# Two weight tiles side by side after each norm, one-column root sums, and the scan's preparation shared between VectorE and GpSimd

## The reference, cut to what matters

```python
def rms_norm(x, g):
    y = x * lax.rsqrt(jnp.mean(x * x, axis=-1, keepdims=True) + NORM_EPS)
    return y * g
h = rms_norm(x, g_pre_mix[l]) * (1.0 + sc1) + sh1
y, yc = token_mixer(h, hc, p, rope_hd, rope_mla, not last)
x = x + gt1 * rms_norm(y, g_post_mix[l])
h = rms_norm(x, g_pre_mlp[l]) * (1.0 + sc2) + sh2
x = x + gt2 * rms_norm(sq_relu_mlp(h, w_mlp1[l], w_mlp2[l]), g_post_mlp[l])
```

```python
w_log = -softplus(-(w0[d] + wt @ w2[d])) - 0.5;  decay = exp(-exp(w_log))
a = sigmoid(a0[d] + al @ a2[d])
kk = heads(k * k_k[d]);  kk = kk / max(norm(kk), 1e-12)
kd = heads(k * (1.0 + (a - 1.0) * k_a[d]))
dirs.append((decay, kd, -kk, kk * a))
```

## Time and profile before

| what | value |
|---|---|
| median of 3 runs | 2324.39 us (2322.61 to 2325.31) |
| the profiled execution's own time | 2323.33 us |
| its span | 2321.5 us |
| TensorE busy (matmuls) | 2164.8 us, 93% |
| VectorE, ScalarE, GpSimd busy | 959.0, 672.5, 804.5 us |
| mean granted TensorE clock | 0.974 of full |

### The profile page before, as it was taken

One profiled execution on the slowest core, in us unless ns is written; L12 is line 12 of the kernel. 1 busy time (PEld: TensorE's weight loads), 2 busy tenths in 40 slices (PEclk: granted clock), 3 DMA queues, 4 the chain that ended last, 5 costly groups with the idle time before them and its releaser, 6 DMA issues.

```text
span 2321.5 us, 44921 instructions
## 1 busy us (share of the span) xinstructions
PE 2164.8 (93%) x19332; PEld 1761.0 (76%) x19332; DVE 959.0 (41%) x1442; ACT 672.5 (29%) x1186; POOL 804.5 (35%) x566
## 2 busy tenths in 40 slices
PE   5999899979898999999999899989989988999997
PEld 3888477658776888888888678847759866888886
DVE  3002355476644622414142510335486646352452
ACT  3110366642312211102111321046642323221221
POOL 3333243032144223232332543235213154444444
PEclk9999999989999999999999999999989999999998
DMA  7221200120022122222223331120120033333331
GB/s 268 83 73 55 73 2 2 61 74 4 25 70 100 55 64 64 63 63 63 63 63 136 100 119 54 38 74 1 61 73 4 12 93 119 99 94 95 93 97 63
DMA packets 45433, 163.23 MB, mean 70 GB/s; under 512 B 5505, under 2 KB 5505, under 8 KB 45025
## 3 DMA queue, kind: packets, MB, share of 16 engines
q1 hardware_dynamic: 44480, 158.29, 21.2%
q0 software_dynamic: 800, 2.69, 0.3%
HBM read 158.86 MB, written 2.10 MB: 69 GB/s over the span
## 4 chain that ended last, share of the span: by engine, by line
PE 83%; DVE 8%; ACT 4%; issue 2%; DMA 1%; POOL 1%; SPq 1%; DVEq 0%; ACTq 0%; POOLq 0%
PE ps L1489 79%; PE ps L1812 3%; DMA flat<-wmod_dram 1%; DVE part_h L1089 1%; DVE hT L1082 1%; ACT flat L795 1%; PE ps L2080 1%; DVE part_h L1358 0%; DVE flat L1473 0%; POOL xT L572 0%; POOL flat L562 0%; ACT flat L958 0%; DVE flat L1282 0%; ACT flat L959 0%; DVE flat L1291 0%
## 5 line engine op out<-in xcount | busy, mean ns | idle before, releaser
L1489 PE MATMUL ps<-part_hi,wparts 128*128 128x512 f32 (+1 forms) x3072 | 825.2, 355 | 20.4 <-DVE part_h L1089 7.4
L1489 PEld LDWEIGHTS ps<-part_hi,wparts 128*128 128x128 f32 x3072 | 548.6, 191 | 111.6 <-DVE part_h L1089 12.2
L543 POOL TENSOR_TENSOR wparts<-flat,wparts 128x1024 fp32r<-128x1024 f32 x184 | 446.8, 2428 | 524.6 <-ACT wparts L1004 518.9
L1489 PE MATMUL ps<-part_h,wparts 128*128 128x512 f32 (+1 forms) x1536 | 544.1, 354 | 0.0
L1489 PE MATMUL ps<-flat 64*64 64x32 f32 (+8 forms) x8200 | 420.9, 258 | 27.8 <-DVE flat L1303 10.6
L1489 PE MATMUL ps<-part_mlp,wparts 128*128 128x512 f32 (+1 forms) x1536 | 414.1, 357 | 15.0 <-DVE part_h L1089 9.1
L1489 PEld LDWEIGHTS ps<-flat 64*64 64x64 f32 (+4 forms) x8200 | 323.7, 142 | 112.6 <-issue 75.0
L1489 PEld LDWEIGHTS ps<-part_h,wparts 128*128 128x128 f32 x1536 | 295.1, 192 | 39.9 <-issue 1.6
L1004 ACT ACTIVATE wparts<-flat 128x1024 fp32r<-128x1024 f32 x112 | 118.8, 1061 | 695.0 <-PE ps L1489 695.0
L1489 PEld LDWEIGHTS ps<-part_mlp,wparts 128*128 128x128 f32 x1536 | 274.6, 190 | 58.8 <-POOL wparts L543 10.1
L1489 PE MATMUL ps<-part_lo,wparts 128*128 128x512 f32 (+1 forms) x768 | 272.2, 354 | 0.0
(11 more groups left out here) (210 smaller groups left out, 2052.8 us busy)
## 6 DMA issues: line engine op xcount, KB each, us to landing
flat<-w_dram SPq DMA_DIRECT2D x128, 512.0 KB, 3.6
flat<-wmod_dram SPq DMA_DIRECT2D x88, 512.0 KB, 5.6
flat<-win_dram SPq DMA_DIRECT2D x40, 512.0 KB, 3.6
flat<-wout_dram SPq DMA_DIRECT2D x16, 512.0 KB, 3.7
hT<-wmod_dram SPq DMA_DIRECT2D x8, 512.0 KB, 7.7
xT<-xT_dram SPq DMA_DIRECT2D x8, 384.0 KB, 6.6
flat<-rope_dram SPq DMA_DIRECT2D x2, 1024.0 KB, 5.5
out_dram<-xT SPq DMA_DIRECT2D x8, 256.0 KB, 2.1
```

The source lines that it names most:

```text
L543: pool.tensor_tensor(wlo[q % 2], src, whi[q % 2], ALU.subtract).then_inc(s_used[q], 1)
L1489: return pe.matmul(out, lhsT, rhs, start=start, stop=stop)
```

## The change

1. `product` takes several tiles: after a norm the first two tiles (three in the input projection of the last layer) are computed side by side as the pieces come. A third pair of weight parts (`wspare`, slot 2) lies in the work area. `IN_SLOT`, `MLP_SLOT` and `MLP_AFTER` give each tile its slot and what its split waits for. In the MLP GpSimd makes the high part of the first three tiles of an iteration instead of two, and ScalarE's high part of tile n waits for tile n-3. TensorE's loops are written out.
2. All roots have the narrow form: `tile_sums` multiplies each block of 128 squares by one column of ones; `token_sums` is gone. For the first norm of the last layer VectorE adds squares 4 and 5, and 6 and 7, so that six pieces are summed.
3. The two tail rows of the modulation are loaded behind the scan into the work area (`tail_slabs`) and not through the ring; both are taken ahead of the sums (`tail_row`).
4. In `post` VectorE's own pieces are scaled into PSUM and added from there.
5. The scan's preparation: GpSimd makes `bh`, the sum for the bonus and most of `RV`; the backward running sums are taken over the reversed tokens, without the difference and sum; the gate's matmuls, its copies and the ring rows are moved; VectorE tells after `bh`, `nkk` and `kd[0]` (`s_prep` counts to 3), and TensorE begins `paired` with that and with GpSimd's `s_side`, `keyed` with the second count.

```diff
+SPARE = 2
+IN_SLOT = (0, 1, SPARE) + tuple((n - 3) % 2 for n in range(3, NZ))
+MLP_SLOT = (0, 1, SPARE) * 4 + (0, 1, 0, 1)
+MLP_AFTER = (None,) * 3 + tuple(n - 3 for n in range(3, 14)) + (12, 13)
+POOL_HI = 3
...
-                stream(wmod_d, (MOD_FROM[l] + MOD_MIX) * SLOTS, MOD_TAIL * SLOTS)
+                for x in range(2):
+                    sp.wait_ge(s_y[x], answered(l, STEPS))
+                for k in range(MOD_TAIL * SLOTS):
+                    sp.dma_start(tail_slabs[k], wmod_d[(MOD_FROM[l] + MOD_MIX) * SLOTS + k, :, :]
+                                 ).then_inc(s_mod[2 + k // SLOTS], 16)
...
+            def in_splits(l):
+                for n in range(NZ):
+                    if n < 2:
+                        pool.wait_ge(s_tile[2 + n], TILES * l + 1)
+                    elif n == 2:
+                        pool.wait_ge(s_modmm, next_done(1) if l else MOD_FIRST)
+                    else:
+                        m = n - 3 if n < 5 else n - 2
+                        pool.wait_ge(s_tile[m % SLOTS], TILES * l + m // SLOTS + 2)
+                    split(n % SLOTS, F_IN[l] + n // SLOTS, IN_SLOT[n])
...
-                pool.wait_ge(s_prep, 5 * l + 5)
+                for n in range(4):
+                    pool.wait_ge(s_kkn, 8 * l + n + 1)
+                    pool.wait_ge(s_rpe, 12 * l + n + 3)
+                    pool.tensor_tensor(bh[:, n, :], nkk[:, n, :], aa[:, n, :], ALU.mult).then_inc(s_side, 1)
+                for f in range(2):
+                    pool.wait_ge(s_kkn, 8 * l + f + 7)
+                    pool.tensor_tensor(bonus_in[:, f, :], kd[:, f, :], kd[:, 2 + f, :], ALU.add).then_inc(s_side, 1)
+                pool.wait_ge(s_used[SLOTS - 1], F_OUT[l] + 1)
+                pool.wait_ge(s_ex, 8 * (l + 1))
+                pool.tensor_tensor(cells(-1, RV, [64, 2], [256, CTX // CH], C1),
...
+                for v, b in enumerate(BACKWARD):
+                    ins = pool.tensor_tensor(cells(-1, RV + v * 512 + P, [64, 2], [256, 2], C1),
...
+                    if v == 1:
+                        ins.then_inc(s_side, 1)
+                ch.link(ins)
+                pool.wait_ge(s_prep, 3 * (l + 1))
+                ch.link(pool.memset(cells(-1, state(0, 0), [1, 256]), 0.0))
...
                     for n in range(2, 2 * KT):
...
-                        nc_.activation(whi[q % 2], slab[:, q * SLAB:(q + 1) * SLAB], ACT.Copy).then_inc(s_whi, 1)
+                        if n >= POOL_HI:
+                            m = MLP_AFTER[n]
...
+                            act.wait_ge(s_tile[m % SLOTS], 1 + i * 4 + (TILES * l + T_MLP + m // SLOTS + 1))
+                            nc_.activation(whi[MLP_SLOT[n]], slab[:, q * SLAB:(q + 1) * SLAB], ACT.Copy).then_inc(s_whi, 1)
                         if k < KT:
...
+                            act.wait_ge(s_tile[k % SLOTS], 1 + i * 4 + (TILES * l + T_MLP + k // SLOTS + 1))
...
                     else:
-                        ch.link(ins)
-                        V.tensor_tensor(xv[:, k, 0:t], xv[:, k, 0:t], yT[:, k, 0:t], ALU.add).then_inc(s_xup, 1)
+                        if own:
+                            dve.wait_ge(*summed(l, which // 2, own[-1]))
+                        own.append(k)
+                        for s, a, b in segs(l, True):
+                            ins = scaled_tile(k, a, b, ps[:, own_at[s]:own_at[s] + b - a])
+                        ch.link(ins)
+                        for s, a, b in segs(l, True):
+                            ins = V.tensor_tensor(xv[:, k, a:b], xv[:, k, a:b], ps[:, own_at[s]:own_at[s] + b - a], ALU.add)
+                        ins.then_inc(s_xup, 1)
...
+                    V.tensor_tensor_scan(cells(-1, CS[n] * TOK + at, [step, TOK]), smask,
+                                         cells(-1, F_WORK + W_SG + n * TOK + at, [step, TOK]), 0.0,
+                                         ALU.mult, ALU.add).then_inc(s_cs, 1)
...
                     for k in range(KT):
                         pe.wait_ge(ready[0], ready[1] + k)
-                        for a, b in spans:
-                            ins = part(k, a, b)
-                return ins
+                        for o, q, slot, fill in tiles:
+                            if k == 0:
+                                pe.wait_ge(s_used[q], fill + 2)
+                            for a, b in spans:
+                                ins = part(o, slot, k, a, b)
+                            if k == KT - 1:
+                                ins.then_inc(s_tile[q], 1)
...
-                    for a, b in ((0, LAT), (LAT, TOK)) if which == 0 or l < LAST else ((0, LAT),):
-                        ins = mm(ps[:, SUMS + a:SUMS + b], ones, sq[:, k, a:b], k == 0, k == KT - 1)
+                    for b in range(nb):
+                        ins = mm(ps[:, NS + b:NS + b + 1], sq[:, k, b * P:(b + 1) * P], ones[:, 0:1],
+                                 k == 0 and b == 0, k == end - 1 and b == nb - 1)
...
-                ring_row(1)
+                for n in range(MOD_TAIL):
+                    tail_row(l, n)
                 tile_sums(l, 2, 0, KT)
-                ring_row(4)
                 spread_root(l, 2)
...
-                pe.wait_ge(s_prep, 5 * l + 5)
+                pe.wait_ge(s_rpe, 12 * (l + 1))
+                pe.wait_ge(s_prep, 3 * l + 1)
+                pe.wait_ge(s_side, 7 * (l + 1))
```

358 lines of the change are left out of this document (198 added, 160 removed).

## The result

| | before | after |
|---|---|---|
| median | 2323.5 us (4 runs, 2319.44 to 2325.31) | 2290.89 us (4 runs, 2288.44 to 2294.09) |
| the profiled execution | 2323.33 us, span 2321.5 | 2289.43 us, span 2287.4 |
| mean granted TensorE clock | 0.974 | 0.974 |

The ratio is 0.986, 95% interval 0.9846 to 0.9873: faster by 1.3 to 1.5%. The forecast was 2284.4, range 2271 to 2300. The direction and the places were right; the sum was 6.5 us too good.

The account below looks back on a forecast made before the run. TensorE was taken to bound the kernel, its matmuls busy 93% of the span, so gains come only where it waits. Terms summed to 40.0 us off 2323.33: 2283.3, or 2284.4 by the median; range 2271 to 2300.

Parts of the forecast that it names:

- Layer 0's MLP norm: Ahead of layer 0's MLP: spread root 1.2 us earlier, two tiles end sooner, 3.6 off for the clock; gain 9.5 us.
- 48 matmuls are 96 records, 11.4 us: Ahead of layer 0's MLP: the one-column sums take 0.118 us a record, 11.4 us in all.
- clock rival: One-column sums leave TensorE at half clock through the side-by-side stretch; 2324 us, or 2343 with following tiles slow; chance 0.04.
- Between the layers: Ahead of layer 1's input projection: spread root 3.2 us earlier, three tiles run with the pieces; gain 10.4 us.
- I take 1.3 off (0 to 3): Between the layers: 1.3 us deducted because VectorE's two additions of squares stand beside GpSimd's splits.
- Layer 1's MLP norm: Ahead of layer 1's MLP: norm stays put, first matmul no longer waits for the slab's split; gain 3.8 us.
- The MLP of layer 1: Four iterations each lose a 0.67 us wait for the last `h1` low part; gain 2.7 us.
- Scan preparation: Before each layer's scan: TensorE starts at 494 and the first inverse level at 504.9 in layer 0; gain 2.9 us, twice.
- the tail, 10.9 us: Scan preparation: from TensorE's start to the first inverse level takes 10.9 us, where it was 8.6.
- lock rival: Scan preparation: VectorE and GpSimd take turns throughout, so scan terms are 0 or below; 2290 us; chance 0.17.
- half rival: Side-by-side tiles give half: about 20 of 25 us of the norms' tiles shrink to 10; 2298 us; chance 0.12.
- what would show it: Signs listed beforehand: two tiles in 17 to 18 us, spread roots about -1, -3 and 0 us, certain waits gone.

Follow-up runs that it names:

- e11_filler4: The changed kernel with four unused 512-column matmuls behind each of the first seven pieces of the sums ahead of layer 0's MLP: 2311.69 us, one run.
- e5: The changed kernel with VectorE's own post-norm pieces scaled in place in SBUF again instead of into PSUM, then added: 2297.62 us, ratio 0.9897.
- e12: The changed kernel with GpSimd's two additions for the bonus held until VectorE's four running sums are done: 2289.83 us, ratio 0.9862.
- e4: The changed kernel with the six products for the backward blocks moved from GpSimd back to VectorE: 2288.22 us, ratio 0.9851.
- e1: The changed kernel with its tiles one after the other again, only one taking the pieces as they come: 2310.5 us, ratio 0.9934.

## Why the prediction was right, and where its terms were not

- **Start** (5.4, measured 5.9): right. 4.6 of it is the pair of tiles, as seen at the third tile; the rest is a wait of 1.09 for ScalarE behind the fourth tile which the forecast didn't name.
- **Layer 0's MLP norm** (9.5, measured 6.6): the pieces, the splits and the two tiles went as worked out. The step that failed is "48 matmuls are 96 records, 11.4 us", with its clock: the price came from 24 records behind full-speed work. The clock rival was about this, but in the wrong place: the text let the clock fall *behind* the sums and took 3.6 us for it; it fell 3.7 us into them and made them 18.1 us long, 6.7 more than counted; the modulation rows ended 1.6 sooner, so the spread root came 5.0 after its forecast. The earlier trace rows showed the same stretch at 0.50 before the wide sums began. In the profile after it came back under the two modulation rows (0.66 from 710 to 715, 1.00 from 715 to 720), and in e11_filler4 it stayed at 1.00 with wide records among the sums; what had brought it back before the change was not tested by itself.
- **Between the layers** (10.4, measured 6.1): the step that failed is "I take 1.3 off (0 to 3)" for the two additions. They cost 2.7 more than alone, the 2.32 us instruction still stood ahead of them, and the last sums ran at half clock: the spread root gained 0 instead of 3.2. The three tiles and the 2 us wait for the fourth were right (2.32).
- **Layer 1's MLP norm** (3.8, measured 4.9): the split was not waited for, but the number came out by two errors of opposite sign. The spread root was 1.3 us late, so the first matmul gained 2.2 and not 3.8, and the forecast booked nothing for what follows it, where 2.4 us were gained (12.0 us for the two tiles instead of 14.5, which had begun at half clock).
- **The end** (2.4, measured 2.2): right, with the cause shown by e5.
- **The MLP of layer 1** (2.7, measured 1.7): the four waits are gone from TensorE's table, each worth 0.67; 1 us of them was given back in stretches where no row shows a wait, which stays open.
- **Scan preparation** (2 x 2.9, measured 2.5 and 1.1): the start of TensorE came within 1 us, and the choice to let two of four running sums wait (3.6 us) measured 3.1 (9.88 against 4 x 1.69 = 6.76), with the cause shown by e12. The Trainium skill (SBUF — State Buffer, Who interferes with whom) says it of any VectorE instruction with two SBUF inputs beside a GpSimd instruction that reads SBUF; for products, additions, running sums and for the PSUM operand, which stays out of it, rows of this case now agree. Mis-sized was the tail, 10.9 us: 11.9 in layer 0, where the masks took 6.8 us and not 5.2 and `chunk_keys` began 1.1 late, and 13.4 in layer 1, where the further 1.5 are clock; from its first `kd` product to its last `nkk` one VectorE takes 26.9 us in both layers.
- **The lock rival** (0.17) named e4's finding for six of the products, the **half rival** (0.12) is refuted by e1, and the **clock rival** (0.04) gave the sums' share without its end: the clock was back at 741, ahead of the first tile's matmul.
- Of **what would show it**, these came: two tiles in 17 to 18 us (17.0 ahead of layer 0's MLP), no wait for the low parts, none for a split or the last `h1` part in layer 1, a wait of 2.32 for the fourth tile's split, a running sum of 3.36. The spread roots did not: +3.8, 0 and +1.3 us instead of about -1, -3 and 0. The granted clock of 0.5, which the forecast named as a sign of being wrong, did come, in the sums and not in the tiles.
- The terms missed in sum 9.0 us (40.0 less 31.0), and 3.1 came by chance from clock dips. That the time lay inside the range is partly luck and partly its width of 29 us: the two largest misses, 2.9 and 4.3 us, went the same way, and the terms that came out right were in one case (layer 1's MLP norm) two errors that cancelled.
